# The first six weight splits of two expert stages given to ScalarE and GpSimd, ahead of the routing's end

## The reference, cut to what matters

```python
# first block: 16 experts, each takes its 128 best tokens (expert choice)
aff   = softmax(h2 @ moe_router)                  # [1024, 16]
# for each expert: its 128 tokens with the largest aff
a     = x_e @ moe_w_gate[e]; b = x_e @ moe_w_up[e]       # 1024 x 1024
y_e   = (silu(a) * b) @ moe_w_down[e] * gate_e           # added back to its tokens

# second block: 4 groups x 8 experts, each token takes its 2 best of one group
# assignments sorted by expert, padded to blocks of 128 rows, one expert a block
a     = x_b @ w_expert_gate[e]; b = x_b @ w_expert_up[e]  # 1024 x 512
y_b   = (silu(a) * b) @ w_expert_down[e] * gate_b         # 512 x 1024, added back
```

## Time and profile before

| | |
|---|---|
| median of 3 runs | 2179.3 us (2179.16 to 2180.51) |
| the profiled execution, its own time | 2180.93 us |
| its span, first to last instruction | 2179.3 us |
| granted PE clock, mean | 0.973 of full |
| PE busy | 2030.7 us (93%) |
| DVE busy | 1672.9 us (77%) |
| ACT busy | 1240.9 us (57%) |
| POOL busy | 467.9 us (21%) |
| DMA | 592.47 MB, mean 272 GB/s |

### The profile page before, as it was taken

One profiled execution on the slowest core, in us unless ns is written; L12 is line 12 of the kernel. 1 busy time (PEld: TensorE's weight loads), 2 busy tenths in 40 slices (PEclk: granted clock), 3 DMA queues, 4 the chain that ended last, 5 costly groups with the idle time before them and its releaser, 6 DMA issues.

```text
span 2179.3 us, 32240 instructions
## 1 busy us (share of the span) xinstructions
PE 2030.7 (93%) x9821; PEld 1685.3 (77%) x9821; DVE 1672.9 (77%) x1890; ACT 1240.9 (57%) x1460; POOL 467.9 (21%) x367
## 2 busy tenths in 40 slices
PE   3999999969999999999699999999999999999993
PEld 2888888857888878787577787888888888878872
DVE  5676755478999999999545455447999999999994
ACT  4311103207878787877533533223888888888873
POOL 2000001101011111111100353110344443433443
PEclk9999999959999999999899999999999999999997
DMA  9277754528999999999711112345999999999994
GB/s 344 89 249 242 244 189 165 198 102 317 381 378 389 380 387 381 386 382 385 262 44 47 41 39 106 126 174 192 395 382 383 376 370 379 377 374 365 367 333 155
DMA packets 234180, 592.47 MB, mean 272 GB/s; under 512 B 23938, under 2 KB 61078, under 8 KB 234108
## 3 DMA queue, kind: packets, MB, share of 16 engines
q1 hardware_dynamic: 207808, 518.06, 63.8%
q0 software_dynamic: 22640, 61.31, 9.6%
q10 hardware_dynamic: 3660, 12.17, 1.5%
HBM read 560.57 MB, written 50.91 MB: 281 GB/s over the span
## 4 chain that ended last, share of the span: by engine, by line
PE 50%; DMA 23%; DVE 11%; SPq 6%; issue 5%; ACT 3%; POOL 1%; ACTq 0%; DVEq 0%; POOLq 0%
PE ps L2156 15%; PE ps L2159 14%; PE ps L2157 14%; DMA ring<-in_w_expert_up 13%; DMA ring<-in_moe_w_down 7%; SPq L534 5%; DVE mL L2043 2%; DVE mL L1646 2%; DMA ring<-in_ada_w 1%; ACT mH L1292 1%; PE ps L2291 1%; PE ps L2435 1%; DVE xz L1792 1%; PE ps L2164 1%; PE ps L2253 1%
## 5 line engine op out<-in xcount | busy, mean ns | idle before, releaser
L2043 DVE TENSOR_TENSOR mL<-ring,mH 128x1024 fp32r<-128x1024 f32 x384 | 480.0, 1291 | 25.1 <-ACT mH L1292 24.4
L1646 DVE TENSOR_TENSOR mL<-ring,mH 128x1024 fp32r<-128x1024 f32 x384 | 454.8, 1222 | 33.8 <-ACT mH L1107 25.2
L1107 ACT ACTIVATE mH<-ring 128x1024 fp32r<-128x1024 f32 x384 | 402.2, 1063 | 100.8 <-PE ps L2159 61.2
L1292 ACT ACTIVATE mH<-ring 128x1024 fp32r<-128x1024 f32 x384 | 398.6, 1058 | 64.7 <-DMA ring<-in_w_expert_up 32.1
L2156 PE MATMUL ps<-mH,xsH 128*128 128x512 f32 x1072 | 428.7, 400 | 4.1 <-DVE mL L2043 2.4
L2159 PE MATMUL ps<-mH,xsL 128*128 128x512 f32 x1072 | 419.3, 391 | 0.0
L2157 PE MATMUL ps<-mL,xsH 128*128 128x512 f32 x1072 | 417.4, 389 | 0.0
L2156 PEld LDWEIGHTS ps<-mH,xsH 128*128 128x128 f32 x1072 | 201.6, 188 | 44.0 <-issue 3.3
L2159 PEld LDWEIGHTS ps<-mH,xsL 128*128 128x128 f32 x1072 | 201.2, 188 | 43.7
L2157 PEld LDWEIGHTS ps<-mL,xsH 128*128 128x128 f32 x1072 | 201.7, 188 | 38.7
L2156 PE MATMUL ps<-mH,hidH 128*128 128x512 f32 x536 | 213.6, 399 | 9.9 <-DVE hidL L1691 7.4
(11 more groups left out here) (419 smaller groups left out, 3187.2 us busy)
## 6 DMA issues: line engine op xcount, KB each, us to landing
ring<-in_w_expert_gate SPq DMA_DIRECT2D x140, 512.0 KB
ring<-in_w_expert_up SPq DMA_DIRECT2D x140, 512.0 KB
ring<-in_w_expert_down SPq DMA_DIRECT2D x140, 512.0 KB
ring<-in_moe_w_gate SPq DMA_DIRECT2D x128, 512.0 KB
ring<-in_moe_w_up SPq DMA_DIRECT2D x128, 512.0 KB
ring<-in_moe_w_down SPq DMA_DIRECT2D x128, 512.0 KB
ring<-in_ada_w SPq DMA_DIRECT2D x96, 512.0 KB
ring<-in_sc_w_in SPq DMA_DIRECT2D x24, 512.0 KB
```

The lines of the kernel that those rows point to most:

```text
L1107: act.activation(mH[:, m % WSETS, :], ring[:, m % RING, :], ACT.Copy).then_inc(S["m1_hi"], 1)
L1292: act.activation(mH[:, wset, :], ring[:, slot, :], ACT.Copy).then_inc(S["m2_hi"], 1)
L1646: dve.tensor_tensor(mL[:, m % WSETS, :], ring[:, m % RING, :], mH[:, m % WSETS, :].bitcast(F32), ALU.subtract).then_inc(S["m1_lo"], 1)
L2043: dve.tensor_tensor(mL[:, wset, :], ring[:, slot, :], mH[:, wset, :].bitcast(F32), ALU.subtract).then_inc(S["m2_lo"], 1)
```

## The change

In both stages the first six chunks (the six sets) are split by ACT and Pool. ACT writes the six high parts ahead of `row_copy("_2")` in stage 1, and behind the routing's last Exp and the load of `final_row` in stage 2. Pool writes the six low parts with a new `early_lo`: in stage 1 it stands behind `store_rows` and ahead of the first gather, in stage 2 behind the constants of the routing and ahead of the wait for the token tables. Each waits for its high part and then signals the semaphore that DVE signalled. DVE, at the first six chunks, only waits for the six signals, and splits from the seventh chunk on.

```diff
@@ -729,6 +729,12 @@
                                     out_offset=bass.IndirectOffsetOnAxis(ap=tok_out[r][:, 0:1], axis=0)
                                     ).then_inc(y_added[r], 16)
 
+        def early_lo(hi, lo, m):
+            pool.wait_ge(S[hi], m + 1 + past.get(hi, 0))
+            pool.tensor_tensor(mL[:, m, :], ring[:, m, :], mH[:, m, :].bitcast(F32), ALU.subtract).then_inc(S[lo], 1)
+
+        for m in range(WSETS):
+            early_lo("m1_hi", "m1_lo", m)
         gather(0, 0)
 
         def m1_step(q, r):
@@ -885,6 +891,8 @@
                 settle(pool)
             scatter_rows(ys[r], tok_out[r]).then_inc(m2_out[r], 16)
 
+        for m in range(WSETS):
+            early_lo("m2_hi", "m2_lo", m)
         pool.wait_ge(S["rows_known"], 2)
         for e in range(2):
             tokens_known(0, e)
@@ -1111,6 +1119,8 @@
             act.activation(xsH[:, r, 4 * j:4 * j + 4, :].rearrange("p a b -> p (a b)"), ps[:, 6 + j, :],
                            ACT.Copy).then_inc(S["m1_xT_hi"], 1)
 
+        for m in range(WSETS):
+            m1_split(0, m, False)
         row_copy("_2")
         act.wait_ge(S["slots_ready"], 1)
         for j in range(2):
@@ -1131,7 +1141,8 @@
                 if m == 21 and not (static(q) and e == E1 - 1):
                     for j in range(2):
                         x_hi(e + 1, 1 - r, j)
-                m1_split(e, m, m1_waits(q, r, m))
+                if m1_waits(q, r, m):
+                    m1_split(e, m, True)
 
         in_pairs(act, E1, m1_step)
 
@@ -1291,6 +1302,9 @@
                 act.wait_ge(S["m2_used"], n - WSETS + 1 + past["m2_used"])
             act.activation(mH[:, wset, :], ring[:, slot, :], ACT.Copy).then_inc(S["m2_hi"], 1)
 
+        for c in range(WSETS):
+            m2_hi(0, 0, c)
+
         def x_hi2(e, r, j):
             act.wait_ge(S["m2_xT"], 2 * e + j + 1 + past["m2_xT"])
             act.activation(xsH[:, r, 4 * j:4 * j + 4, :].rearrange("p a b -> p (a b)"), ps[:, 7 - j, :],
@@ -1328,7 +1342,7 @@
                                    ACT.Copy).then_inc(S["m2_hT_hi"], 1)
                 if c in (9, 11) and not (static(q) and s >= E2):
                     x_hi2(s + 1, 1 - r, (c - 9) // 2)
-                if not (static(q) and s == E2 and c < 8):
+                if not (static(q) and (s == 0 and c < WSETS or s == E2 and c < 8)):
                     m2_hi(q, r, c)
             if static(q) and s == 0:
                 for j in range(2):
@@ -1693,7 +1707,10 @@
                 if m == 21 and not (static(q) and e == E1 - 1):
                     for j in range(2):
                         x_lo(e + 1, 1 - r, j)
-                m1_split(e, m)
+                if not m1_waits(q, r, m):
+                    dve.wait_ge(S["m1_lo"], WSETS)
+                else:
+                    m1_split(e, m)
 
         in_pairs(dve, E1, m1_step, steps, 2)
         y_out(E1 // 2 - 1, 1)
@@ -2095,7 +2112,9 @@
                     x_lo2(s + 1, 1 - r, (c - 9) // 2)
                 if c == 11 and static(q) and s == E2 - 1:
                     hidden(s, r)
-                if not (static(q) and s == E2 and c < 8):
+                if static(q) and s == 0 and c < WSETS:
+                    dve.wait_ge(S["m2_lo"], WSETS + past["m2_lo"])
+                elif not (static(q) and s == E2 and c < 8):
                     m2_lo(q, r, c)
             if static(q) and s == 0:
                 for j in range(2):
```

## The result

The changed kernel takes 2207.4 us (median of 4 runs, 2204.7 to 2208.2), the kernel before in runs beside it 2179.2 us (4 runs, 2178.0 to 2180.5). The ratio is 1.0123, with a 95% interval of 1.0111 to 1.0135: slower by 24 to 29 us. The profiled execution spans 2206.0 us against 2179.3, so there are 26.7 us to be found in the traces. The forecast was 2205, in a range of 2187 to 2213.

A forecast was written before the change was run, and what follows sets the result against it. Each stage's end was taken to be set by when and how long the weight stream runs, then by PE's start. Stage 1's 9 plus stage 2's 16.6 gave 25.6 us on 2179.3, so 2205, range 2187 to 2213.

The forecast's parts named there:

- its two terms: The costs forecast for the two stages: +9 us in stage 1 and +16.6 us in stage 2.
- Stage 1, the way to PE's start: Stage 1: Pool's six subtractions delay the gather 14 us; PE starts its first expert at 515.4, 15.5 us late.
- Stage 1, the stream: Stage 1 weight loads: 6.5 chunks, 8.9 us, behind, and DMA full from then on; +9 us.
- Stage 2, the port: Stage 2 routing: Pool's subtractions and DVE's two-input operations exclude each other for whole instructions; routing 13.5 us late.
- Stage 2, the clock: Stage 2: PE rests 13 us, its clock falls, and its first 6.2 us run at half speed; +3.1 us.
- the six low parts' early end: Stage 2: PE starts 1.2 us earlier but loses it again waiting later; price 0 (bound -1.2).
- the mis-sized term: Stage 1's forecast cost, from the weight stream falling behind: +9 us.
- A: Rival: the routing of stage 2 is not held up, only stage 1 pays; 2188 us, chance 0.13.
- B: Rival: Pool's subtractions take 3.02 us each, not 2.39; +3.8 us in both stages, 2212 us, chance 0.12.
- C: Rival: six chunks split and slots refilled before PE starts save 8.2 us of DMA; 2171 to 2179, chance 0.03.
- nothing competes on DVE there: Stage 1, beside Pool's six subtractions: DVE only waits for the gathered rows, so Pool's 2.39 us each stands.

The follow-up runs named there:

- experiment 3: Kernel before with the change in stage 1 only, Pool's six subtractions moved ahead of the store of rowsT: 2175.7 us, ratio 0.9981.
- experiment 4: Kernel before with the change in stage 1 only, the first gather moved ahead of Pool's six subtractions: 2180.9 us, ratio 1.0006.
- experiment 6: Kernel before with stage 2 changed, but Pool writes zeros to the six low parts instead of subtracting: 2179.4 us, ratio 1.0001.
- Experiment 7: Changed kernel with more filler products on PE in both waits, 68 in stage 1 and 54 in stage 2: 2201.4 us, 1.0101 of the kernel before.
- experiment 1: Kernel before with the change in stage 1 only, stage 2 as before: 2194.0 us, ratio 1.0063.
- experiment 2: Kernel before with the change in stage 2 only, stage 1 as before: 2195.8 us, ratio 1.007.
- experiment 5: Kernel before, but in stage 2 ACT writes six high parts early and DVE the low parts while awaiting gathered rows: 2179.7 us, ratio 1.0001.

## Why the prediction was right, and what hides in the sum

The forecast of the time was right, and so were the causes that it named in both stages. One step was not: how the stream of stage 1 goes on once PE has started. Of its two terms neither was exact, they erred in opposite directions, and that the sum came so close is in part luck.

**Stage 1, the way to PE's start: right, with small errors that cancel.** Pool's six took 13.86 us, 2.31 each, where 2.39 was taken. The gather came 14.7 us later (14 forecast; 0.7 us of that lies ahead of the change, since the store itself stands at 491.01 instead of 490.29; why is open, and the other runs have it between 489.55 and 491.35). The rows landed 5.7 us behind the gather instead of 4.6; a chunk's load had been issued 0.5 us ahead of the gather, where experiments 3 and 4 have none so near and take 4.6, but no run tests that alone. From the transposes to PE's first product it took 4.0 us instead of the forecast 5.6, since the clock came back while the fillers ran: it is 0.50 up to 514 us and 0.74 from 514 to 515, 2.9 us behind the first transpose where the prediction had taken 6.2. PE starts at 515.63; 515.4 was forecast, against 500.03 before. Experiments 3 and 4 show that the place on Pool is the cause.

**Stage 1, the stream: this is the step that failed.** "It is 6.5 chunks, 8.9 us, behind, and DMA is full from then on." The first half is right. Here are the two windows of before that answer to the first and third after:

```profile
490.00:500.00 10.00, 6.92 (x51) 6.56 (x50) 3.47 (x10) 3.40 (x5) 1.59 (x2) 0.89 0.18 54
...
520.00:540.00 20.00, 20.00 (x95) 16.61 (x95) 19.59 (x22) 16.78 (x19) 2.94 (x2) 1.00 1.05 388
```

From 490 to 520 us before had moved 0.54 + 7.08 = 7.62 MB, after it is 1.15 + 3.08 = 4.23 MB: 3.4 MB less, 8.9 us at 383 GB/s. But in the next 20 us it is 388 GB/s against 305, another 1.7 MB or 4.3 us. Together 13.2 us; from 540 to 640 us the rates are nearly alike (383 and 381). Stage 2's constants came 14.1 us late, of which 0.7 lie ahead of the change: 13.4. The term was 9. PE's side says the same: from its first product to stage 2's constants it took 1.5 us less than before (967.1 after 968.6), where the prediction had it 6 shorter, because PE's gaps from 640 to 1040 us hardly shrank, from 7.4 to 5.9 us.

What DMA lacks is chunks that are issued ahead of it. SP before, from PE's start on: 4 + 8 + 6 chunks in 20 us, 1.14 us apart at first, while DMA in that time moved 12.5 (the line of the eight is the first below). After, SP stands from 505.8 to 519.80 and then issues one chunk every 1.36 us. SP's queue before, and then after in narrow windows:

```profile
504.51 8.28 SPq L534 DMA_DIRECT2D ring<-in_moe_w_down  x8
...
503.14 2.64 SPq L534 DMA_DIRECT2D ring<-in_moe_w_down  x2
...
519.80 2.97 SPq L534 DMA_DIRECT2D ring<-in_moe_w_down  x3
```

ACT's splits have the same step, 518.73, 520.09, 521.45 and so on, each with an idle time that a PE product ends. The mechanism that the rows speak for: before, PE started with one set filled, and the splits ran ahead of it into five empty ones at their own pace, freeing slots faster than DMA filled them, so loads queued up. After, PE starts with all six sets full. A slot comes free only when PE has finished a chunk, 1.36 us, which is just the time of a load, and no queue builds up until 530 us, where the issues come 1.13 us apart. Experiment 3 has the same dip without any delay of the gather (288 and 376 GB/s), so it belongs to the full sets, not to the late start. Experiment 4, where Pool had written only two sets when PE started, has 314 and 384 GB/s in the same windows, behind 160 from 490 to 500, and so no dip behind 520 us. This mechanism is read from the traces; no run varies the number of full sets and nothing else. In the change it is paid on top of the lost time, in experiment 3 it eats half of the gain.

**Stage 2, the port: right, 12.4 us instead of 13.5.** The last of the masks and ranks' operations went from 1478.37 to 1504.92, which is 26.55, less the 14.13 by which the stage began later: 12.4. DVE got a little more done between Pool's instructions than the "less than 1 us" of the prediction: in the 14.1 us it did what alone takes 14.1 - 12.4 = 1.7. Experiment 6 shows that the pace of these operations of DVE hangs on Pool's reading, as far as its 5.6 us go. The Trainium skill (SBUF — State Buffer, Who interferes with whom) says that a VectorE instruction with two SBUF inputs contends with a GpSimd instruction that reads SBUF, not with one that only writes; by that rule the trace agrees, 7.55 us against 1.55.

**Stage 2, the clock: right, 2.5 us instead of 3.1.** It is what is left of the 14.9 us between constants and gather: 0.8 us from the last mask to the first filler (the ranks' products take 1.22, 1.06 and 0.47 us for 0.60, 0.59 and 0.30), 1.85 in the 88 fillers, and 0.15 less behind them. The clock stayed at 0.50 for about 6 us from the first of these products on, as forecast, but that product starts 0.24 us behind the start of the last mask's operation, where before, behind fillers, it was 0.60. Experiment 7 takes 3.0 back. Together stage 2 costs 14.9; 16.6 was forecast.

**The rest.** The sum 0.7 + 13.4 + 14.9 is 29.0, and the span grew by 26.7. From the gather of stage 2 to the end it is 2.3 us less than before. I don't read a gain into it. The same stretch of stage 2, from the gather to the end of the span, is 683.1 us in the kernel before, 680.2 in experiment 1, 682.6 in experiment 3 and 681.0 in experiment 4, while the change has 680.8 and experiment 2 has 683.5. It differs by 3 us between traces in which the code of stage 2 is the same, and experiment 5 gives 0 for the six low parts' early end, as the prediction did.

So it is luck that the forecast of 25.6 us misses the 26.7 of the spans by only 1.1 us: four errors cancel, 4.4 us too little in stage 1 (the mis-sized term), 1.7 too much in stage 2, 0.7 from ahead of the change, and 2.3 of scatter the other way (4.4 - 1.7 + 0.7 - 2.3 = 1.1).

**The rivals.** A, the routing of stage 2 isn't held up: refuted by experiment 2 and the timeline. B, subtractions of 3.02 us: they took 2.31 and 2.35, output type and DVE notwithstanding. C, the head start wins: it does when PE starts on time, in experiment 3, and by 4.1 us; the 8.2 us that the prediction counted for it are there and half of them go in the dip.

## What to carry to other kernels

Work given to an idle engine inherits the place in that engine's program: ask what it stands behind (a store that waits for the end of a chain) and what stands behind it (the gather on which everything hangs), since two lines exchanged made 13.7 us into nothing, and six moved over one store made them a gain of 4.1. Moving subtractions from DVE to Pool while DVE is in a dense chain of small operations with two inputs cost DVE nearly Pool's whole time here (12.4 of 14.1 us), and a rest of PE on top; beside the rounds of top-8 the same six cost it nothing, and done by DVE itself, in a wait of its own, they did no harm either. A head start in full buffers was worth half its length here: with every buffer full the consumer's pace sets the issues, and the queue that kept DMA at its rate has to form again.

## What the runs showed of the hardware that was not expected

A DVE instruction with one input was held up too, and for all six of Pool's subtractions at once. In the changed kernel's stage 1, DVE's timeline shows it, between two neighbours of the same kind and size:

```profile
490.93 0.17 DVE L1651 SCALAR_TENSOR_TENSOR pick<-pick,ps 128x16 f32<-128x16 f32 x1
491.13 0.17 DVE L1653 TENSOR_TENSOR slot_gate<-best,ps 128x16 f32<-128x16 f32 x1
491.34 14.11 DVE L1654 CAST slot_tok<-pick 128x16 uint32<-128x16 f32 x1
505.48 0.15 DVE L1670 COPY tok_in<-slot_tok 128x1 uint32<-128x1 uint32 x1
```

The cast of 16 elements began 0.22 us ahead of Pool's first subtraction and ended at 505.45, 0.03 us behind the last (505.42); in experiment 4, without Pool's subtractions beside it, it took 0.17 us. (By that it would have ended 0.05 us ahead of Pool's recorded start; Pool's spans are rough, and why it had not ended by then isn't shown.) The prediction said that nothing competes on DVE there, which is wrong. It made no difference to the time, since the gather stands behind the same six on Pool, but a gather issued from another queue would have been as late: its token numbers come out of this cast. In stage 2 one operation with two inputs got through for each of Pool's instructions, each taking 2.1 to 2.5 us until it ended; the cast wasn't let through at any of the five boundaries. Why the two differ is open. In experiment 6 the two one-input operations held up by Pool's writes (0.45 us for 0.17 and 1.01 us for 0.18) can't have met a reading of Pool's, so they fit a contention for writing; the cast may be of that kind, but stood beside reads and writes both. The Trainium skill (SBUF — State Buffer, Who interferes with whom) has casts and TENSOR_SCALAR among the operations that can, with operands that meet its conditions, take the port pair shared with GpSimd, and says that whichever of the two comes second is then blocked for a whole instruction of the other; by that rule the trace agrees that they contend, but the cast's 14.11 us are six of Pool's instructions and not one.

Pool's subtraction with an fp32r output took 2.31 us (six in 13.86) and beside DVE's masks 2.35 (six in 14.10): nearly all of the loss between these short DVE instructions and Pool's long ones fell on DVE.
